# Both attentions as flat sequences, the first head by head, with part of the wide steps on GpSimd

## The reference, cut to what matters

```python
# layer 0: 8 heads, two score maps each; keys = 1024 tokens + 256 context tokens
s = einsum('bqhmd,bkhmd->bhmqk', qb, kk) * scale
p = softmax(s, axis=-1)
a = p[:, :, 0] - lam * p[:, :, 1]
o = einsum('bhqk,bkhe->bqhe', a, vv)
y = (rmsnorm(o, sub_g) * (1 - lam_init)).reshape(...) @ wo
# context tokens attend to the context keys alone
# layer 1: 16 query heads in 4 groups; 128 queries see a window of 3 blocks of 128 keys
# (2 at the edges) and the 256 context keys; the softmax has one more logit, the sink
p = softmax(concat([s_loc, s_ctx, sink]))[..., :-1]
y = (p_loc @ v_loc + p_ctx @ v_ctx).reshape(...) @ wo
```

## Time and profile before

| | us |
|---|---|
| median of 3 runs (3390.61 to 3397.22) | 3397.03 |
| profiled execution | 3395.04 |
| its span | 3393.2 |
| TensorE busy in the span | 2917.1 (86%) |
| VectorE busy | 1286.9 (38%) |
| ScalarE busy | 814.1 (24%) |
| GpSimd busy | 548.0 (16%) |

### The profile page before, as it was taken

How to read it: one execution, slowest core, us unless ns; L and a number is a source line. 1 busy time by engine, 2 the same in 40 slices (tenths; PEclk the granted TensorE clock), 3 DMA queues, 4 the chain that set the end, 5 groups by cost and what they waited for, 6 DMA issues and landing times. The chain is left out here.

```text
span 3393.2 us, 38136 instructions
## 1 busy us (share of the span) xinstructions
PE 2917.1 (86%) x13041; PEld 1628.0 (48%) x13041; DVE 1286.9 (38%) x2390; ACT 814.1 (24%) x1819; POOL 548.0 (16%) x767
## 2 busy tenths in 40 slices
PE   7999995999996966999999859968888859999982
PEld 3444333888883533444444324457774424443431
DVE  4444112777774243111111165367772341110114
ACT  2211002766673000000000043145551000000000
POOL 2455100111112110000000035400001100000000
PEclk8999997999998977999999979989999869999996
DMA  6333668322225328999999383254443289999985
GB/s 240 97 99 130 223 232 195 65 50 43 49 49 183 132 89 348 416 387 413 384 413 391 150 297 118 62 114 91 90 113 134 95 362 422 426 427 426 427 378 207
DMA packets 256876, 760.81 MB, mean 224 GB/s; under 512 B 31216, under 2 KB 176544, under 8 KB 220656
## 3 DMA queue, kind: packets, MB, share of 16 engines
q1 hardware_dynamic: 152160, 642.51, 50.6%
q10 hardware_dynamic: 89296, 78.90, 7.4%
q0 software_dynamic: 15296, 37.78, 2.8%
HBM read 678.57 MB, written 98.37 MB: 229 GB/s over the span
## 5 line engine op out<-in xcount | busy, mean ns | idle before, releaser
L1823 PE MATMUL psum<-moe_ring,moe_xT 128*64 128x512 f32 (+1 forms) x2240 | 705.4, 600 | 15.6 <-DMA moe_ring<-in_e_w 13.3
L391 PE MATMUL psum<-qkv_w,act_hT 128*128 128x512 f32 x1376 | 611.8, 598 | 0.1
L1823 PEld LDWEIGHTS psum<-moe_ring,moe_xT 128*64 128x64 f32 (+1 forms) x2240 | 276.4, 161 | 408.8 <-issue 406.8
L391 PEld LDWEIGHTS psum<-qkv_w,act_hT 128*128 128x128 f32 x1376 | 257.0, 192 | 306.9 <-issue 306.9
L1844 PE MATMUL psum<-moe_ring,moe_hT 128*64 128x512 f32 (+1 forms) x1120 | 352.8, 594 | 1.6 <-DVE moe_hT L1924 1.6
L1107 ACT ACTIVATE att_prob<-psum,att_nmax 128x1280 f32<-128x1280 f32 (+3 forms) x288 | 283.8, 986 | 114.3 <-DVE att_nmax L1221 66.9
L1920 DVE TENSOR_TENSOR moe_hh<-psum,moe_sg 128x512 f32<-128x512 f32 x50 | 34.6, 692 | 665.9 <-PE psum L1823 665.9
L1381 PE MATMUL psum<-post_wo,post_oT 128*128 128x512 f32 x576 | 258.1, 603 | 22.3 <-DMA post_wo<-in_a_wo 14.1
L954 PE MATMUL psum<-att_kT,att_q 128*128 128x512 f32 (+1 forms) x832 | 211.5, 391 | 47.7 <-ACTq L1202 26.3
L1221 DVE TENSOR_REDUCE att_nmax<-psum 128x1 f32<-128x1280 f32 (+1 forms) x160 | 204.3, 1278 | 113.6 <-PE psum L954 111.1
L1844 PEld LDWEIGHTS psum<-moe_ring,moe_hT 128*64 128x64 f32 (+1 forms) x1120 | 133.1, 160 | 184.6 <-issue 180.4
(11 more groups left out here) (248 smaller groups left out, 3101.2 us busy)
## 6 DMA issues: line engine op xcount, KB each, us to landing
moe_ring<-in_e_w SPq DMA_DIRECT2D x216, 2048.0 KB, 16.6
ada_w<-in_ada_w SPq DMA_DIRECT2D x48, 1024.0 KB, 6.4
att_q<-qk_d SPq DMA_DIRECT2D x144, 256.0 KB, 4.8
qk_d<-qkv_stg ACTq DMA_DIRECT2D x112, 256.0 KB, 2.5
qkv_w<-in_a_wqkv SPq DMA_DIRECT2D x6, 2048.0 KB, 8.9
prep_y<-y_d SPq DMA_DIRECT2D x10, 1024.0 KB, 6.5
o_d<-att_oTs ACTq DMA_DIRECT2D x18, 512.0 KB, 2.8
post_oT<-o_d SPq DMA_DIRECT2D x18, 512.0 KB, 4.6
```

Source lines behind the costliest of these rows:

```text
L391: ins = nc.tensor.matmul(psum[:, u.par, :], hT[:, k, u.t * P:(u.t + 1) * P], qw[:, u.C % 2, k], start=(k == 0), stop=(k == KD - 1))
L1823: ins = nc.tensor.matmul(psum[part, bank, :], xT[:, 4 * half + k, part], ring[:, w13[x, half] % RING, k, bank * DE:(bank + 1) * DE], start ...
```

## The change

- Both attentions lose their loops. `UNITS0` is head by head: for each head its eight full units and then its two context units. `UNITS1` is tile by tile as before. The pipeline runs through all units of a layer. The loop of the output stage is written out as well.
- Layer 0 loads keys and queries of one head for all tiles (`load_head`), in two buffers. Head 0 is loaded in the front, among the modulation weights; head h when head h-2 has its scores.
- Outputs go into `oT`, which holds all tokens in SBUF; `o_d` and its stores and loads are gone. Layer 1 reads V from `vstg` in SBUF, `v_d` is gone; its keys (`kall`) are loaded whole.
- `wo` is loaded during the last head of layer 0, and at the start of attention 1 in layer 1.
- Layer 0: VectorE mixes the first seven key blocks (`SHARE`) alone. GpSimd does the last three as a scaling and an addition, and the two small steps of the normalisation that VectorE had. TensorE waits for it ahead of the eighth transpose. The second bank is copied by VectorE, not ScalarE.
- Layer 1: VectorE scales the first map, GpSimd the second. TensorE waits for both ahead of the first transpose.

```diff
-    for l, ntrip, t0, kinds, nblk in [(0, TX // 2, 0, ("all", "all"), (10, 10)), (0, 1, TX, ("ctx", "ctx"), (2, 2)),
-                                      (1, 1, 0, ("first", "last"), (4, 4)), (1, TX // 2 - 1, 1, ("mid", "mid"), (5, 5))]:
+    UNITS0 = [(h, t) for h in range(KD) for t in range(TA)]
+    UNITS1 = [(t, j) for t in range(TX) for j in range(KD)]
+    SHARE = 7 * P
...
# SyncE, front of layer 0
             for n in range(11, 48):
                 load_ada(sp, n)
+                if n == 24:
+                    sp.wait_ge(s_qev, 42)
+                    for par in range(2):
+                        sp.wait_ge(s_qst[par], 16 + 32 * 20)
+                    load_head(sp, 0)
...
+    def load_head(sp, h):
+        buf = (h + 1) % 2
+        for part in range(2):
+            for m in range(2):
+                sp.dma_start(kT[buf][64 * part:64 * part + 64, m].bitcast(F32), qk_d[KD + h, part, 64 * m:64 * m + 64, :]).then_inc(s_kq[buf], 16)
+        for rows in range(2):
+            for m in range(2):
+                sp.dma_start(aq0[buf][64 * rows:64 * rows + 64, m].bitcast(F32), qk_d[h, :, 64 * m:64 * m + 64, :].rearrange("x d n -> d x n")).then_inc(s_kq[buf], 16)
+
+    def sp_att0(sp):
+        load_head(sp, 1)
+        for h in range(2, KD):
+            sp.wait_ge(s_score, 2 * TA * (h - 1))
+            load_head(sp, h)
+        sp.wait_ge(s_score, 2 * TA * (KD - 1))
+        load_wo(sp, 0)
...
# GpSimd, layer 0
+        def normal(n):
+            q = n % 2
+            pool.wait_ge(s_sumsq, n + 1)
+            pool.wait_ge(s_mixp, n + 1)
+            poolc.link(pool, nc.gpsimd.tensor_tensor(ssq[:, q], ssq[:, q], epsum[:, q], ALU.add))
+            poolc.link(pool, nc.gpsimd.tensor_tensor(fac[:, q], ssq[:, q], neghalf[:, 0:1], ALU.pow))
+            if n >= 2:
+                pool.wait_ge(s_turn[2], n + 1)
+            nc.gpsimd.tensor_scalar(on[:, q], raw[:, q], fac[:, q], None, ALU.mult).then_inc(s_on, 1)
+
+        for n, (h, t) in enumerate(UNITS0):
+            q = n % 2
+            pool.wait_ge(s_coef, n + 1)
+            ins = nc.gpsimd.tensor_scalar(epsum[:, q], den[:, q, 0:1], den[:, q, 0:1], EPS, ALU.mult, ALU.mult)
+            if t < TX:
+                other = prob0[:, 2 * q + 1, SHARE:]
+                poolc.link(pool, nc.gpsimd.tensor_scalar(other, other, coef[:, q], None, ALU.mult))
+                ins = nc.gpsimd.tensor_tensor(prob0[:, 2 * q, SHARE:], prob0[:, 2 * q, SHARE:], other, ALU.add)
+            ins.then_inc(s_mixp, 1)
+            if n:
+                normal(n - 1)
...
# TensorE, layer 0, one unit
+            pe.wait_ge(s_mix, n + 1)
+            if n:
+                pe.wait_ge(s_took[2], n)
+            if not full:
+                pe.wait_ge(s_mixp, n + 1)
+            blocks(n, 0, 4 if full else 2, 6).then_inc(s_turn[0], 1)
+            if n:
+                pe.wait_ge(s_raw, n)
+            if full:
+                blocks(n, 4, 7, 7)
+                pe.wait_ge(s_mixp, n + 1)
+                nc.tensor.transpose(psum[:, 7, 3 * P:], prob0[:, 2 * (n % 2), SHARE:SHARE + P], ident).then_inc(s_turn[1], 1)
+
+            scores(n + 2, 0)
...
# VectorE, layer 0
-                    dve.wait_ge(s_exp, 2 * (u0 + j) + 2 + 2)
-                    nc.vector.scalar_tensor_tensor(epsum[:, q], den[:, q, 0:1], EPS, den[:, q, 0:1], ALU.mult, ALU.mult)
-                    nc.vector.scalar_tensor_tensor(probs(l, j, 0, 0, width), probs(l, j, 1, 0, width), coef[:, q], probs(l, j, 0, 0, width), ALU.mult, ALU.add).then_inc(s_mix, 1)
+            width = SHARE if full else CTX
+            nc.vector.scalar_tensor_tensor(prob0[:, 2 * q, 0:width], prob0[:, 2 * q + 1, 0:width], coef[:, q], prob0[:, 2 * q, 0:width], ALU.mult, ALU.add).then_inc(s_mix, 1)
...
+            if t < TX:
+                dve.wait_ge(s_turn[1], full_before(n) + 1)
+                nc.vector.tensor_copy(aT0[:, n % 2, 4:8, :], psum[:, 7, :].rearrange("p (b n) -> p b n", n=P)).then_inc(s_took[1], 1)
...
# layer 1: VectorE and GpSimd
-                        for m in range(2):
-                            p = probs(l, j, m, 0, width)
-                            ins = nc.vector.tensor_scalar(p, p, rden[:, q, m:m + 1], None, ALU.mult)
+            nc.vector.tensor_scalar(prob1[:, 2 * q, 0:width], prob1[:, 2 * q, 0:width], rden[:, q, 0:1], None, ALU.mult).then_inc(s_mix, 1)
...
+            pool.wait_ge(s_coef, N0 + n + 1)
+            nc.gpsimd.tensor_scalar(prob1[:, 2 * q + 1, 0:width], prob1[:, 2 * q + 1, 0:width], rden[:, q, 1:2], None, ALU.mult).then_inc(s_mixp, 1)
...
# output stage
-            sp.dma_start(oT[:, par].rearrange("p k n -> p (k n)"), o_d[ds(t, 1)].rearrange("o p n -> p (o n)")).then_inc(s_pin[par], 16)
             sp.dma_start(xt[:, par], src).then_inc(s_pin[par], 16)
-            if isinstance(t, int) and t == 0 and l == 0:
-                load_wo(sp, l)
...
-            pe.wait_ge(s_pin[par], pin_count(T, par))
             pe.wait_ge(s_x1, T + 1)
```

More of the change, by code:

```diff
@@ L176, in tile_steps @@
     def tile_steps(eng, tiles, step, chain=None, links=0):
[L179 to L186, removed]
+        for t in range(tiles):
             step(t, t % 2)
@@ L803, in build @@
     on = A("on", [P, 2, P])
-    oTs = A("oTs", [P, 2, KD, P])
-    KWID = CTX + 3 * P
[L807 to L836, removed]
@@ L853, in at @@
[L853 to L864, removed]
+    nmax = A("nmax", [P, 2, 2])
+    den = A("den", [P, 2, 2])
+    rden = A("rden", [P, 2, 2])
+    mx = A("mx", [P, 2, 2])
+    es = A("es", [P, 2, 2])
+    KWID = CTX + 3 * P
+    A = Arena("att1")
@@ new lines, in sp_att0, with load_q @@
+    def sp_att0(sp):
[5 more added lines that the diff above has]
+        load_wo(sp, 0)
+    def load_q(sp, t, half):
+        src = qk_d[4 * half:4 * half + 4, :, :, t * P:(t + 1) * P]
+        for rows in range(2):
+            for m in range(2):
+                sp.dma_start(aq1[64 * rows:64 * rows + 64, half, m].bitcast(F32).rearrange("d u x n -> d (u x) n"),
+                             src[:, :, 64 * m:64 * m + 64, :].rearrange("u x d n -> d (u x) n")).then_inc(s_aq[half], 16)
@@ new lines, in sp_att1 @@
+    def sp_att1(sp):
+        load_q(sp, 0, 0)
+        for part in range(2):
+            for m in range(2):
+                sp.dma_start(kall[64 * part:64 * part + 64, m:4:2].bitcast(F32), qk_d[8:10, part, 64 * m:64 * m + 64, :].rearrange("h d n -> d h n")).then_inc(s_kq[0], 16)
+        load_q(sp, 0, 1)
+        load_wo(sp, 1)
+        for t in range(1, TX):
+            for half in range(2):
+                sp.wait_ge(s_score, 2 * N0 + 2 * (8 * (t - 1) + 4 * half + 4))
+                load_q(sp, t, half)
@@ new lines, in pe_att0, with scores, blocks @@
+    def pe_att0(pe):
+        def scores(n, m):
+            if n >= N0:
+                return
+            h, t = UNITS0[n]
+            buf = (h + 1) % 2
+            if t == 0 and m == 0:
+                pe.wait_ge(s_kq[buf], 128 * (h // 2 + 1))
+            if n:
+                pe.wait_ge(s_exp, 2 * (n - 1) + m + 1)
+            for b, (lo, hi) in enumerate(((0, 512), (512, 1024), (1024, 1280)) if t < TX else ((SEQ, NTOK),)):
+                for x in range(2):
+                    ins = nc.tensor.matmul(psum[:, 3 * m + b, 0:hi - lo], aq0[buf][:, m, x, t * P:(t + 1) * P], kT[buf][:, m, lo:hi], start=x == 0, stop=x == 1)
+            ins.then_inc(s_score, 1)
+        def blocks(n, lo, hi, bank):
@@ L1305, in build @@
-    s_pw = [sem("s_pw0"), sem("s_pw1")]
+            pe.wait_ge(s_took[1], FULL0 + n + 1)
+            for b in range(nb):
+                if b == 4:
+                    pe.wait_ge(s_took[2], N0 + 1 + n + 1)
+                v = vstg[:, TX + b if b < TC else keys[b - TC], j // 2 * HD:(j // 2 + 1) * HD]
+                for m in range(2):
+                    ins = nc.tensor.matmul(psum[64 * m:64 * m + 64, 7, 0:P], v, aT1[:, n % 2, 2 * b + m, :], start=(b == 0), stop=(b == nb - 1))
+            ins.then_inc(s_av, 1)
```

657 lines of the change are left out of this document (255 added, 402 removed).

## The result

The changed kernel takes 3435.64 us (median of 4, 3433.68 to 3437.19) against 3397.03: ratio 1.0118, 95% interval 1.0100 to 1.0136. It is 1.2% slower; the prediction said 3366 and faster, and its range ended at 3425. The profiled span goes from 3393.2 to 3433.4 us.

| stretch, from landmark to landmark | before | after | difference | predicted |
|---|---|---|---|---|
| to SyncE's first load of attention 0 | 538.46 | 552.94 | +14.5 | +4 |
| from there to the first mix | 30.08 | 9.01 | -21.1 | -21 |
| first to last mix | 480.2 | 510.3 | +30.1 | +2 |
| last mix to first output product | 19.76 | 6.54 | -13.2 | -14 |
| from there to front 1's last product | 1137.60 | 1136.86 | -0.7 | 0 |

What follows compares the result with a forecast made beforehand. Attention units were bound by a ring of waits, with TensorE nearly full. Front +4, attention 0 start -21 and body +2, output stages -14 and -8, attention 1 +6 sum to -31: 3366 us; likeliest range 3345 to 3395, 8-in-10 range 3298 to 3425.

Steps and rivals of the forecast that it cites:

- GpSimd's price: GpSimd's scaling in both attentions: 1.5 ns for each column beyond 128, so 1.0 us for 384 columns.
- rival 1: GpSimd in both attentions dearer than 2.2 ns a column, kernel not faster; about 3436 at 3.06 ns; chance 0.20.
- 43 us for each ns: Both attentions: the sum moves 43 us per ns a column of GpSimd's one-input work, reaching zero at 2.2 ns.
- Layer 0's ring of 6.97: Attention 0: chain of waits through GpSimd sets a full unit's period at 6.97 us, against 5.90; +51 in all.
- Layer 1's 5.26 and 4.58: Attention 1: periods of five-block and four-block units with GpSimd's scaling, +0.26 and +0.65 us a unit; +13 and +10.
- The flat part: The change apart from GpSimd's wide work, such as trip borders and load holes going in both attentions: -105 forecast.
- -69 + 20: Attention 0's body: trip borders and load holes go, -69; head by head order with narrow context units costs +20.
- 0 at the start: Start of attention 1: whole key load replaces windows of about the same bytes ahead of the first unit, no change.
- The lead of 7: Front of layer 0: three weight buffers give an estimated lead of 7 against an 11 us block; stall 4 us.
- Rival 2: Both attentions: VectorE and GpSimd hardly disturb each other, 65 us less than the forecast, about 3301; chance 0.13.
- Rival 3: GpSimd's one-input work in both attentions goes at the fill's rate, 0.88 ns a column: about 3341; chance 0.20.
- Rival 4: Attention 0: flat order gives nothing, holes return as waits for per-head loads: 3435; chance 0.05 together with mishaps.

Runs made afterwards that it cites:

- the flat version: Changed kernel with layer 0's mix and layer 1's scaling both back on VectorE, no wide attention step on GpSimd: 3275.25 us, ratio to the kernel before 0.9647.

## Why the prediction was wrong, point by point

**GpSimd's price: the step that failed.** "For the columns beyond 128 I take 1.5, half-way between the fill and the two-input slope". They cost 2.49 ns, above the 2.2 at which the sum was said to be zero, and the prediction had named that as a sign of being wrong. The mechanism was right and this term of it was mis-sized. The argument for the low price, "a two-input operation costs 2.1, and one input should not cost more", is false here: the addition of two tensors goes at (992 - 452) / 256 = 2.11 ns and the scaling by a per-partition scalar at 2.49. The 0.611 of the earlier trace rows had the answer half hidden: 0.32 of it was columns.

**The agreement with rival 1 is luck.** Rival 1 gave 3436, and 3435.6 was measured, but its 3436 belongs to 3.06 ns. With 2.49 the prediction's own 43 us for each ns give 3366 + 43 = 3409: slower, as measured, but inside the stated range. The rest came from terms that rival 1 didn't have. Of the 71 us between forecast and result, 32 are the two rings (7 in layer 0, 25 in layer 1), 12 the last two full units of each head, 7 the lower clock at head changes, 10 the front, 4 the start of attention 1; some 3 are the intervals around the context units, and the remaining 2 or 3 are small differences of the other rows.

**How far GpSimd reached.** Layer 0's ring of 6.97 came out at 7.11: the scaling took 1.25 for 1.0, but the steps between GpSimd's operations took less than was set for them. Layer 1's 5.26 and 4.58 came out at 5.67 and 4.91, which the price explains (2.24 for 0.4 + 1.38). But "1.07 more than 5.90 for six units of each head" left out the last two full units (5.48 + 5.48 where VectorE alone gives 5.38 + 4.12), and the comparison was with the ring of before, not with what the rest of the change would have given. Forecast for all of GpSimd's wide work: 51 + 23 = 74 us; measured 160, 79 in layer 0 and 82 in layer 1. Of the 82, 28 are a gain of the flat version that GpSimd's ring hid.

**The flat part: -105 forecast and -119 measured, in part by luck.** The start of attention 0 gave -21, right. Layer 0's body without GpSimd takes 429.5 us against 480.2, so -51 for -69 + 20. The four intervals around the context units measure 19.6 us where 19.4 was forecast. The output stages gave -13.2 and -6.8 for -14 and -8, right. Three things were missed, and they partly cancel. In layer 1 the wait for the last copied blocks moves from block 0 to block 4 of the V product; the prediction put the period of 5.00 down to ScalarE's chain beside the ring and didn't read this line, worth -28. Without that gain the flat version is worth -91 (3303.6 against 3395.0), 14 short of the forecast: some 10 in the front, and 4.4 at the start of attention 1, where "0 at the start" was forecast although all keys now came ahead of the first unit.

**Front: a second step that failed.** "365 at a full share: the block takes 11 us" put the rate of the modulation weights on head 0's loads. These move 218 GB/s at a full share, so 3.9 MB take 18 us, and TensorE waited 11.13. The lead of 7 is what is left of 18; no run measured it by itself. The lower clock behind the wait adds about 2.

**What remains of layer 0's body.** Six of the seven intervals that follow a head change are 8.23 in place of 7.11. Two of them (busy time by stretch, granted clock, DMA share and GB/s last), and the scores in the second (timeline):

```profile
625.70:632.81 7.11, 4.86 (x37) 4.20 (x36) 5.22 (x7) 4.48 (x10) 4.78 (x6) 1.00 1.02 216
...
689.42:697.65 8.23, 5.99 (x34) 5.12 (x33) 5.22 (x8) 4.48 (x10) 4.78 (x6) 0.79 1.03 215
```

```profile
693.28 2.48 PE L892 MATMUL psum<-att_kT,att_q 128*128 128x512 f32 x6
```

Both have full DMA queues; only the longer one has a granted clock below 1.00, and so it is in all six. Its six score matmuls take 2.48 us where they take 1.40 in the unit above, after TensorE has waited 1.54 us for GpSimd's addition. So the clock costs the 1.1 us, and not the loads. With the context units apart one interval of 7.37 in place of 5.75 had a clock of 0.77 and no transfer at all (share 0.00). With the same loads and no wait for GpSimd (both steps on VectorE) the seven intervals are 5.75 at a clock of 1.00. Why one head change in the changed kernel escapes is not shown.

**Contention.** The mix and GpSimd's work were set one behind the other, 1.05 + 0.3 = 1.35 us before the scaling; 1.36 was measured. The Trainium skill says this as a rule (SBUF — State Buffer, "SBUF: two separate sides": the port pair is held for a whole instruction). The trace agrees: a one-column product lasts 1.23 us beside a mix of 1.15, 1.63 beside one of 1.55 (the version with both steps on VectorE), and 0.56 beside a context unit's of 0.48. Rival 2 fell with that.

Rival 3, the fill's rate, fell too: VectorE scales 640 columns in 0.51 us (half of the pair's 1.02 in the earlier trace rows) and GpSimd, alone, in 1.89. The Trainium skill (GPSIMD Engine Reference, "Engine selection") calls one-input work roughly line rate; for this operation the measurement says otherwise. Rival 4 fell: TensorE never waits for a head's load behind the first.

## What to carry to other kernels

Before work goes to a second engine, price it there by two widths of the same operation, with the same kind of operands; one width and another operation's slope missed the point at which this change turned. Then ask where its wait stands: three blocks waited for ahead of the next scores cost 79 us, two waited for behind them nothing (how much of this is the place and how much the third block was only estimated). Compare with what the rest of the change gives without the second engine, not with the kernel before. And read every wait that a rewrite moves by a few lines: one in layer 1 was worth 28 us, a quarter of the whole gain of the flat version.

## What the runs showed of the hardware that was not expected

- GpSimd, float32, 128 partitions, while VectorE does no work on SBUF beside it: a per-partition scaling costs 0.29 us + 2.49 ns a column (five widths, 128 to 640), an addition of two tensors 2.11 ns a column beyond 128 (452, 734 and 992 ns for 128, 256 and 384).
- GpSimd waits for VectorE's work on SBUF (640 columns take 2.24 us beside it and 1.89 alone), but VectorE's maximum read from PSUM keeps its 1.49 us beside GpSimd's scaling (599.40 above; also 1.49 on average in the kernel before, where GpSimd has no such step).
- TensorE's granted clock fell in some of the intervals at a head change and not in others of the same work (0.79 against 1.00), and cost 1.1 us each time.
- Loads of keys and queries from `qk_d` with 5 KB rows fill the queues at 218 GB/s (share 1.02), where the modulation weights move 223 at a share of 0.61. The rate doesn't follow the length of the rows: the first queries and keys of attention 1 in the changed kernel, the queries in rows of 512 bytes, move 213 GB/s at a full share (2224 to 2239), and the output weights, in rows of 2 KB, move 390 (1010 to 1017). What the slow ones have in common is that each transfer writes 64 partitions; the fast ones write 128. They also differ in their source, and no run changed the partitions alone.
